# Two transformer blocks in float32 on one core: GpSimd sums the squares of tiles 0 to 13 for the four wide norms

## Chip, cores and metric

One Trainium2 chip, one core. The time is the device time of one launch in microseconds (us), measured from outside; a profiled execution also has a span, from its first to its last instruction. Lower is better.

## What is computed

A sequence of 256 tokens of width 2048 passes through two blocks, all in float32. The first has an RMS norm, an input projection, sparse attention beside a gated convolution, an output projection, a second RMS norm and a convolutional feed-forward part. The second has an RMS norm, latent and differential attention, gates, an output projection, an RMS norm and a gated feed-forward part. A last RMS norm closes the program. The part that matters here:

```
def rms_norm(x, g):
    xf = x.astype(jnp.float32)
    y = xf * lax.rsqrt(jnp.mean(xf * xf, axis=-1, keepdims=True) + NORM_EPS)
    return (y * g.astype(jnp.float32)).astype(x.dtype)

x = x + jnp.concatenate([attn, conv], axis=-1) @ w_out[l]
h = rms_norm(x, ffn_norm_g[l])
x = x + conv_glu_ffn(h, w_up[l], ffn_conv_w[l], ffn_conv_b[l], w_down[l])
...
return rms_norm(x, final_norm_g)
```

For each token the squares of 2048 values are added up. There are four such sums after large products: k = 1 (after `w_out`), k = 3 (after the first block's last down projection; two sums here, since the first block's final norm and the second block's first norm follow each other and are evaluated together), k = 4 (after `w_out_2`) and k = 5 (the last norm, after the second down projection).

## The kernel before

**Layout.** Activations stand transposed: channels on the 128 partitions, tokens along the free dimension. `x` is 16 tiles of 128 channels by 256 tokens. A matrix product is kept exact by splitting: each weight is `w_hi` + `w_lo` and each activation is a pair of halves side by side (`hp` or `yp`, 512 columns). One step of a product, called a pair below, is a 512-column product with `w_hi` (L1585) and a 256-column product with `w_lo` (L1586).

**The stream of weights.** Weights come in units of 128 x 1024 or 128 x 768 values. SyncE's queue loads a unit into one of four `w_raw` buffers, ScalarE copies it to `w_hi` (L540), VectorE (in the first phases GpSimd, L860) subtracts to get `w_lo` (L875), TensorE multiplies. Semaphores hand the four buffers round. TensorE's order is written out by phase (`gemm`, L1596): a step has two groups of output chunks, each group walks `nu` units, and `between` or `hooks` names work put ahead of unit `u` of group `g`.

**The wide norms.** The gains are applied before the sum is known, and the reciprocal root is multiplied in later, so that the next product need not wait. In the closing phase before each norm (`w_out`, `down1_2`, `w_out_2`, `down2_2`), VectorE adds each finished pair of chunks to `x` (L1241, L1242), ScalarE squares the pair of tiles into `sq` (L599; for k = 3 also `sq_g`, L602) and scales them for the next product (L604), VectorE forms the low half (L927, not for k = 5). All engines follow their own program order.

**The sum of squares** is TensorE's. A product with a 128 x 128 block of squares as the stationary operand and one column of ones gives 128 tokens' sums over 128 channels; it adds into columns of PSUM bank `STAT`. That is two products for each tile (`stats`, L1630; product at L1640), each issued as two instructions, after one 4-column product with zeros that starts the sum (L1633, also two instructions). Tiles 0 to 11 are read in `early` (L1616), hooked ahead of group 1, unit 0 of the last step of the closing phase; tiles 12 to 15 in `opening` (L1652), ahead of unit 1 of the next phase. For k = 5 `early` also transposes three pieces of the output (`out_turn`, L1623, transposes at L1561), and tiles 12 to 15 follow the last product. From the sum VectorE and ScalarE make the reciprocal root (`inverse_root`, L962, L593), and TensorE spreads it over the partitions (`spread`, L1645, L1650).

## Time and profile before

| | us |
|---|---|
| median of 3 runs (2957.24 to 2966.63) | 2958.05 |
| profiled execution, its own time | 2957.51 |
| its span | 2955.7 |
| TensorE busy in the span | 2898.1 (98%) |
| VectorE, ScalarE, GpSimd busy | 2092.1, 1375.9, 174.1 |

The span is 1.8 us shorter than the time of the same execution. TensorE is busy nearly throughout, so the question at each place is what it is busy with, and what it would wait for if that work went away. GpSimd works only in the first tenth of the span. A mean clock of 0.985 of full speed was granted to TensorE.

### The profile page before, as it was taken

What the parts mean: (1) busy time and instruction counts of PE and PEld (TensorE: products, weight loads), DVE (VectorE), ACT (ScalarE), POOL (GpSimd) and SP (SyncE); (2) the same over time, 40 slices, a digit from 0 to 9 for tenths busy, and PEclk for the clock granted to TensorE, in tenths of its full rate; (3) what the DMA queues carried; (4) which work ended last, traced back from release to release, by engine and by line L of the source; (5) the groups of instructions that cost most, each with busy time, mean ns of one, the idle gap of its engine ahead of it and who ended that gap; (6) DMA issues with size and microseconds to landing.
All of it is one profiled execution on the core that took longest, in us unless ns stands there. A gap on an engine that the chain in (4) does not pass through costs nothing.

```text
span 2955.7 us, 50070 instructions
## 1 busy us (share of the span) xinstructions
PE 2898.1 (98%) x17096; PEld 2528.0 (86%) x17096; DVE 2092.1 (71%) x3291; ACT 1375.9 (47%) x1798; POOL 174.1 (6%) x81
## 2 busy tenths in 40 slices
PE   6998999999999999999999999999999999999998
PEld 5877888888888888888888888888888888888887
DVE  4986767876886786577776777777657766775674
ACT  3334746644554455445443454544445533343344
POOL 3865000000000000000000000000000000000000
PEclk9999999999999999899999999999999999999998
DMA  9655355665655555444556555555555566565553
GB/s 227 176 145 133 91 136 175 187 192 187 187 189 191 186 185 180 131 135 145 150 167 185 166 173 166 173 167 183 188 162 187 183 196 189 181 197 190 180 183 120
DMA packets 596731, 507.37 MB, mean 172 GB/s; under 512 B 90123, under 2 KB 594715, under 8 KB 596251
## 3 DMA queue, kind: packets, MB, share of 16 engines
q1 hardware_dynamic: 595040, 503.61, 56.6%
q0 software_dynamic: 560, 2.12, 0.2%
q8 instruction: 55, 0.90, 0.1%
q10 hardware_dynamic: 1035, 0.40, 0.1%
q14 instruction: 41, 0.34, 0.0%
HBM read 503.88 MB, written 2.12 MB: 171 GB/s over the span
## 4 chain that ended last, share of the span: by engine, by line
PE 92%; DVE 4%; ACT 2%; issue 1%; ACTq 0%; DMA 0%; DVEq 0%
PE banks L1585 57%; PE banks L1586 28%; PE banks L1640 2%; PE banks L1561 1%; DVE banks L1069 1%; ACT hp_f L660 1%; DVE arena L891 1%; PE banks L1903 0%; PE banks L1659 0%; PE banks L1956 0%; ACTq L520 0%; DVE hp_f L1160 0%; DVE arena L1187 0%; PE banks L1763 0%; PE banks L1906 0%
## 5 line engine op out<-in xcount | busy, mean ns | idle before, releaser
L1585 PE MATMUL banks<-hp,w_hi 128*128 128x512 f32 x4416 | 1567.2, 400 | 13.0 <-issue 10.0
L540 ACT ACTIVATE w_hi<-w_raw 128x1024 fp32r<-128x1024 f32 (+2 forms) x960 | 996.5, 1044 | 1193.4 <-PE banks L1586 1176.5
L875 DVE TENSOR_TENSOR w_lo<-w_raw,w_hi 128x1024 fp32r<-128x1024 f32 (+2 forms) x889 | 1061.3, 1206 | 567.6 <-ACT w_hi L540 550.0
L1586 PE MATMUL banks<-hp,w_lo 128*128 128x256 f32 x4416 | 1236.8, 280 | 0.0
L1585 PEld LDWEIGHTS banks<-hp,w_hi 128*128 128x128 f32 x4416 | 833.3, 189 | 211.5 <-issue 12.3
L1585 PE MATMUL banks<-yp,w_hi 128*128 128x512 f32 x2752 | 965.2, 397 | 4.1 <-DVE yp L1296 2.8
L1586 PEld LDWEIGHTS banks<-hp,w_lo 128*128 128x128 f32 x4416 | 836.8, 189 | 2.6 <-issue 1.9
L1586 PE MATMUL banks<-yp,w_lo 128*128 128x256 f32 x2752 | 767.2, 279 | 0.0
L1585 PEld LDWEIGHTS banks<-yp,w_hi 128*128 128x128 f32 x2752 | 518.3, 188 | 128.0 <-DVE yp L1296 3.8
L1586 PEld LDWEIGHTS banks<-yp,w_lo 128*128 128x128 f32 x2752 | 519.5, 189 | 0.1
L891 DVE TENSOR_REDUCE arena<-banks 128x256 f32<-128x512 f32 (+1 forms) x392 | 251.5, 684 | 86.0 <-PE banks L1586 84.7
L860 POOL TENSOR_TENSOR w_lo<-w_raw,w_hi 128x1024 fp32r<-128x1024 f32 x71 | 171.8, 2423 | 80.5 <-ACT w_hi L540 80.5
L1069 DVE SCALAR_TENSOR_TENSOR banks<-arena,vec,banks 128x256 f32<-128x256 f32 x232 | 102.0, 485 | 3.7
L1585 PE MATMUL banks<-arena_r,w_hi 128*128 128x512 f32 x272 | 101.0, 410 | 1.8 <-DVE arena L891 1.5
L992 DVE TENSOR_TENSOR arena<-arena,cst 128x512 f32<-128x512 f32 x128 | 88.5, 691 | 4.2
L1268 DVE SCALAR_TENSOR_TENSOR arena<-arena,vec 128x256 f32<-128x256 f32 x176 | 77.5, 482 | 17.2 <-ACT arena L722 11.3
L1586 PE MATMUL banks<-arena_r,w_lo 128*128 128x256 f32 x272 | 77.4, 285 | 0.0
L722 ACT ACTIVATE arena<-arena,vec 128x256 f32<-128x256 f32 x88 | 48.2, 595 | 52.7 <-DVE arena L992 52.7
L1241 DVE TENSOR_TENSOR x<-banks,x 128x256 f32<-128x256 f32 (+1 forms) x128 | 53.2, 416 | 23.5 <-PE banks L1586 23.5
L1585 PEld LDWEIGHTS banks<-arena_r,w_hi 128*128 128x128 f32 x272 | 52.3, 192 | 15.8 <-DVE arena L891 4.3
L712 ACT ACTIVATE arena<-arena 128x512 f32<-128x512 f32 x44 | 27.9, 633 | 80.6 <-DVE arena L992 61.4
L787 ACT ACTIVATE arena<-arena,small 128x128 f32<-128x128 f32 x64 | 31.5, 493 | 60.1 <-DVE small L1426 46.2
(255 smaller groups left out, 1565.5 us busy)
## 6 DMA issues: line engine op xcount, KB each, us to landing
w_raw<-in_w_in SPq DMA_DIRECT2D x480, 256.0 KB, 3.0
w_raw<-in_w_up SPq DMA_DIRECT2D x352, 256.0 KB, 2.9
w_raw<-in_w_ffn_up SPq DMA_DIRECT2D x176, 256.0 KB, 3.6
w_raw<-in_w_ffn_gate SPq DMA_DIRECT2D x176, 256.0 KB, 3.0
w_raw<-in_w_down SPq DMA_DIRECT2D x160, 256.0 KB, 3.0
w_raw<-in_w_ffn_down SPq DMA_DIRECT2D x160, 256.0 KB, 3.0
w_raw<-in_w_out SPq DMA_DIRECT2D x128, 256.0 KB, 3.1
w_raw<-in_w_mla_proj SPq DMA_DIRECT2D x64, 256.0 KB, 3.0
```

The costliest lines, as they stand in the source:

```text
L540: nc.scalar.activation(w_hi[:, s, 0:n], w_raw[:, s, 0:n], ACT.Copy).then_inc(hi_ready, 1)
L722: ins = nc.scalar.activation(dst[:, c, :], buf[:, c, FTAPS - 1:], ACT.Identity, scale=vdyn("ffn_conv_w", ch + (FTAPS - 1) * 2 * FT), bias= ...
L860: nc.gpsimd.tensor_tensor(w_lo[:, s, 0:n], w_raw[:, s, 0:n], w_hi[:, s, 0:n].bitcast(f32), ALU.subtract)\
L875: v.tensor_tensor(w_lo[:, s, 0:n], w_raw[:, s, 0:n], w_hi[:, s, 0:n].bitcast(f32), ALU.subtract)\
L891: v.tensor_reduce(dst, pair(b)[0:rows], X, ALU.add).then_inc(chunk_out, 1)
L992: return v.tensor_tensor(dst, dst, bcast(r_row, 2), ALU.mult)
L1069: ins = v.scalar_tensor_tensor(conv_y[:, t, :] if k == TAPS - 1 else acc, src, w, acc, ALU.mult, ALU.add)
L1241: link(v.tensor_tensor(xt, banks[:, c, 0:T], xt, ALU.add))
L1268: ins = v.scalar_tensor_tensor(dst[:, c, :], buf[:, c, k:k + T], vdyn("ffn_conv_w", at_ch[c] + k * 2 * FT), dst[:, c, :], ALU.mult, ALU.add)
L1585: mm(banks[:, b, :], w_hi[:, s, at:at + P], rhs[:, kt, :], start=kt == kt_first, stop=False)
L1586: ins = mm(banks[:, b, 0:T], w_lo[:, s, at:at + P], rhs[:, kt, 0:T], start=False, stop=kt == kt_last)
L1640: ins = mm(banks[:, STAT, at + b:at + b + 1], src[:, t, b * P:(b + 1) * P], ones[:, 0:1], start=False, stop=t == KT - 1, skip_group_check= ...
```

## The change

GpSimd adds, for each of k = 1, 3, 4, 5, tiles 2 and 3, then 4 and 5, up to 12 and 13 into tiles 0 and 1 of `sq`, in place: six additions of 128 x 512, each after the squares of its pair. For k = 3 the same is done for `sq_g`, the two chains by turns, so 30 additions in all. TensorE then reads tiles 0, 1, 14 and 15 alone. For k = 1, 3 and 4 it reads all four in `opening`, after all six additions (semaphore `summed`); `early` has nothing left for them. For k = 5 `early` is moved to unit 3 of group 1, with the transposes first and tiles 0 and 1 behind them, and tiles 14 and 15 follow the last product.

```diff
@@ gpsimd
+            for k in (1, 3, 4, 5):
+                for p in range(1, KT // 2 - 1):
+                    for src, name, done, nth in ((sq, "squares", "summed", NTH[k]), (sq_g, "squares_g", "summed_g", 0))[:2 if k == 3 else 1]:
+                        pool.wait_ge(sem(name), KT // 2 * (nth + 1) + p + 1 if nth or name == "squares" else 2 * p + 2)
+                        if p > 1:
+                            pool.wait_ge(sem(done), (KT // 2 - 2) * nth + p - 1)
+                        nc.gpsimd.tensor_tensor(src[:, 0:2, :], src[:, 0:2, :], src[:, 2 * p:2 * p + 2, :], ALU.add).then_inc(sem(done), 1)
@@ tensor, gemm
-                    step(whole, {(1, 0): lambda: early(k)})
+                    step(whole, {(1, nu - 1): lambda: early(k)})
@@ early
-                stats(k, 0, KT - 4)
                 if k == 5:
                     pe.wait_ge(sem("gained"), KT * NTH[k] + 8)
                     for j in range(3):
                         out_turn(j)
+                    stats(k, (0, 1))
@@ stats
-            def stats(k, t0, t1):
-                if t0 == 0:
+            def stats(k, tiles):
+                if 0 in tiles:
                     mm(banks[:, STAT, 0:4], ident, zeros, start=True, stop=False, skip_group_check=True)
...
-                    for t in range(t0, t1):
-                        pe.wait_ge(sem(name), nth + (t // 2 + 1 if nth else t + 1))
+                    for t in tiles:
+                        if t == 0:
+                            pe.wait_ge(sem(done), (KT // 2 - 2) * (NTH[k] + 1 if at == 0 else 1))
+                        if t == KT - 2:
+                            pe.wait_ge(sem(name), KT // 2 * (NTH[k] + 2) if at == 0 else KT)
@@ opening
-                return {(0, 1): lambda: stats(k, KT - 4, KT), at: lambda: spread(k)}
+                return {(0, 1): lambda: stats(k, (0, 1, KT - 2, KT - 1)), at: lambda: spread(k)}
@@ end
-            stats(5, KT - 4, KT)
+            stats(5, (KT - 2, KT - 1))
```

The first place is the last step of `w_out` on TensorE (k = 1). Before, the products on squares stand between its two groups; `squares` is ScalarE's semaphore, `chunk_out` VectorE's.

```order
L1585 MATMUL banks<-yp,w_hi 128x512
L1586 MATMUL banks<-yp,w_lo 128x256
L1633 MATMUL banks<-small,cst 128x4 [waits chunk_out]
L1640 MATMUL banks<-cst,arena 128x1 [waits squares]
L1640 MATMUL banks<-cst,arena 128x1
L1640 MATMUL banks<-cst,arena 128x1 [waits squares]
```

Now the sum begins behind the first unit of the next phase (L1593 and L1594 are L1585 and L1586 of before, L1641 and L1651 are L1633 and L1640):

```order
L1594 MATMUL banks<-hp,w_lo 128x256
L1641 MATMUL banks<-small,cst 128x4
L1651 MATMUL banks<-cst,arena 128x1 [waits summed]
L1651 MATMUL banks<-cst,arena 128x1 x3
L1651 MATMUL banks<-cst,arena 128x1 [waits squares]
L1651 MATMUL banks<-cst,arena 128x1 x3
L1593 MATMUL banks<-hp,w_hi 128x512 [waits lo_ready3,gained_lo]
```

Twenty-four products went, eight stand there as before, and the start of the sum moved past two units of `w_out` and one of the next phase. The second place is the last step of `down2_2` on TensorE (k = 5), now:

```order
L1594 MATMUL banks<-hp,w_lo 128x256
L1569 MATMUL banks<-cst,arena 128x128 [waits gained]
L1569 MATMUL banks<-cst,arena 128x128 x11
L1641 MATMUL banks<-small,cst 128x4
L1651 MATMUL banks<-cst,arena 128x1 [waits summed]
L1651 MATMUL banks<-cst,arena 128x1 x3
L1593 MATMUL banks<-hp,w_hi 128x512 [waits lo_ready3,mid]
```

Before, the start of the sum, 24 products and the 12 transposes stood ahead of the group's first unit; now 12 transposes, the start and 4 products stand ahead of its last.

On GpSimd the additions follow the last subtraction for the weights; the first rows are k = 1 and the beginning of k = 3:

```order
L860 TENSOR_TENSOR w_lo<-w_raw,w_hi 128x1024 [waits hi_ready] x71
L869 TENSOR_TENSOR arena<-arena 128x512 [waits squares]
L869 TENSOR_TENSOR arena<-arena 128x512 [waits summed,squares] x5
L869 TENSOR_TENSOR arena<-arena 128x512 [waits squares]
L869 TENSOR_TENSOR arena<-arena 128x512 [waits squares_g]
```

Nothing stood behind the subtractions before.

## Rows read from the trace of the kernel before

**Rows 1.** The page: busy time by engine, and the chain that ended last by line.

```profile
PE 2898.1 (98%) x17096; PEld 2528.0 (86%) x17096; DVE 2092.1 (71%) x3291; ACT 1375.9 (47%) x1798; POOL 174.1 (6%) x81
PE banks L1585 57%; PE banks L1586 28%; PE banks L1640 2%; PE banks L1561 1%; DVE banks L1069 1%; ACT hp_f L660 1%; DVE arena L891 1%; PE banks L1903 0%; PE banks L1659 0%; PE banks L1956 0%; ACTq L520 0%; DVE hp_f L1160 0%; DVE arena L1187 0%; PE banks L1763 0%; PE banks L1906 0%
```

**Rows 2.** Timeline, TensorE, k = 1: start us, us, engine, line, operation, count.

```profile
430.01 0.28 PE L1633 MATMUL banks<-small,cst 128*128 128x4 f32 x2
430.15 7.94 PE L1640 MATMUL banks<-cst,arena 128*128 128x1 f32 x48
...
448.71 1.84 PE L1640 MATMUL banks<-cst,arena 128*128 128x1 f32 x16
450.42 0.48 PE L1585 MATMUL banks<-hp,w_hi 128*128 128x512 f32 x1
```

**Rows 3.** Timeline, TensorE, k = 3.

```profile
1176.65 0.28 PE L1633 MATMUL banks<-small,cst 128*128 128x4 f32 x2
1176.79 17.38 PE L1640 MATMUL banks<-cst,arena 128*128 128x1 f32 x96
...
1206.94 3.63 PE L1640 MATMUL banks<-cst,arena 128*128 128x1 f32 x32
1210.43 0.48 PE L1585 MATMUL banks<-hp,w_hi 128*128 128x512 f32 x1
```

**Rows 4.** Timeline, TensorE, k = 4.

```profile
2172.80 0.28 PE L1633 MATMUL banks<-small,cst 128*128 128x4 f32 x2
...
2197.35 0.48 PE L1585 MATMUL banks<-yp,w_hi 128*128 128x512 f32 x1
```

**Rows 5.** Timeline, TensorE, k = 5 and the end.

```profile
2921.29 0.28 PE L1633 MATMUL banks<-small,cst 128*128 128x4 f32 x2
...
2928.82 2.80 PE L1561 MATMUL banks<-cst,arena 128*128 128x128 f32 x12
2931.28 0.78 PE L1585 MATMUL banks<-hp,w_hi 128*128 128x512 f32 x1
...
2941.30 0.95 PE L1640 MATMUL banks<-cst,arena 128*128 128x1 f32 x8
2943.88 1.05 PE L1640 MATMUL banks<-cst,arena 128*128 128x1 f32 x8 [1.64 <-ACT arena L599]
```

**Rows 6.** Windows, TensorE: stretch, length, busy (count), granted clock, DMA share, GB/s.

```profile
430.00:438.00 8.00, 8.00 (x53) 0.68 0.46 141
438.00:443.00 5.00, 5.00 (x16) 0.50 0.12 37
...
448.00:451.00 3.00, 3.00 (x25) 1.00 0.39 117
...
1211.00:1216.00 5.00, 5.00 (x22) 0.66 0.03 10
```

**Rows 7.** Windows, L1585 alone: the count is of pairs; columns as in rows 6.

```profile
700.00:800.00 100.00, 100.00 (x290) 1.00 0.60 188
...
2050.00:2150.00 100.00, 100.00 (x284) 1.00 0.58 187
```

**Rows 8.** One line of GpSimd: count, then min/median/max ns.

```profile
L860 POOL TENSOR_TENSOR w_lo<-w_raw,w_hi x71: 2335/2404/3965, 29.6 to 271.9; 128x1024 fp32r<-128x1024 f32 x71
```

**Rows 9.** Timelines of GpSimd and VectorE, a subtraction beside a VectorE operation, and without.

```profile
262.76 2.39 POOL L860 TENSOR_TENSOR w_lo<-w_raw,w_hi 128x1024 fp32r<-128x1024 f32 x1 [3.66 <-ACT w_hi L540]
...
262.89 4.41 DVE L1185 TENSOR_TENSOR arena<-arena,yp_f 128x2048 f32<-128x2048 f32 x1
...
279.80 2.28 DVE L1192 TENSOR_TENSOR arena<-arena,yp_f 128x2048 f32<-128x2048 f32 x1
```

**Rows 10.** Windows, VectorE, in the closings of k = 1 and 3; columns as in rows 6.

```profile
401.00:423.60 22.60, 18.65 (x33) 1.00 0.85 188
1140.00:1174.00 34.00, 23.83 (x40) 1.00 0.57 179
```

**Rows 11.** Timeline, ScalarE: the squares of the last pair, k = 1.

```profile
448.14 0.63 ACT L599 ACTIVATE arena<-x 128x512 f32<-128x512 f32 x1 [0.88 <-DVE x L1242]
```

More of the change, by code:

```diff
@@ L1628, in out_turn @@
                 ins.then_inc(sem("out_turned"), 1)
-            def stats(k, t0, t1):
-                if t0 == 0:
+            def stats(k, tiles):
+                if 0 in tiles:
                     mm(banks[:, STAT, 0:4], ident, zeros, start=True, stop=False, skip_group_check=True)
-                for src, name, at, nth in ((sq, "squares", 0, KT // 2 * (NTH[k] + 1)), (sq_g, "squares_g", 2, 0)):
+                for src, done, name, at in ((sq, "summed", "squares", 0), (sq_g, "summed_g", "squares_g", 2)):
                     if name == "squares_g" and k != 3:
                         continue
-                    for t in range(t0, t1):
-                        pe.wait_ge(sem(name), nth + (t // 2 + 1 if nth else t + 1))
+                    for t in tiles:
[3 more added lines that the diff above has]
+                            pe.wait_ge(sem(name), KT // 2 * (NTH[k] + 2) if at == 0 else KT)
                         for b in range(QB):
@@ L1641, in stats @@
                                      start=False, stop=t == KT - 1, skip_group_check=True)
-                if t1 == KT:
+                if KT - 1 in tiles:
                     ins.then_inc(sem("sums"), 1)
```

## The prediction

> **What bounds the kernel now.** I read the page first. TensorE is busy 98% of the span, and in the chain that ended last nearly everything is its own: the pairs of L1585 and L1586 make 85%, the products on squares (L1640) 2% [rows 1]. A step that leaves TensorE is thus worth its full length there, if the engine finds its next operands ready. So I read TensorE's timeline at the four norms. At each, the pairs stop and a run of one-column products stands between two of them, with no idle time printed: 48 instructions for k = 1 [rows 2], 96 for k = 3 [rows 3]; k = 4 and 5 are built as k = 1 [rows 4, 5]. The one wait is at the very end, 1.64 us for ScalarE's squares [rows 5].
>
> The reader should see two prices in these rows. The first is the products' own. In the short run behind the next phase's first unit, 16 instructions take 450.42 - 448.71 = 1.71 us, 0.107 us each [rows 2]. In the long run of k = 3, 96 take 17.24 us, 0.180 each [rows 3]. The second price explains the difference: the windows show the granted clock at 0.68 of full speed over the long run of k = 1, and then 0.50, the lower level of 1.2 GHz, for the 5 us after it, though the pairs are back by then [rows 6]. Between 438 and 443 only 16 records of TensorE's products stand, 8 pairs in 5 us, where 14 would fit. Behind the short run the clock is 1.00 [rows 6]. So a long run of one-column products also slows the products of full width that follow.
>
> **What a pair costs.** L1585 stands 290 times in 100 us of a feed-forward phase and 284 times in 100 us late in the second block, both at full clock [rows 7]: 0.345 and 0.352 us for a pair. Where it reads 0.345 and where 0.352 I can't derive. The timeline has the slower pace in all closing steps before the runs, so I use 0.352 there.
>
> **k = 1.** Before, from the start of the sum to the first pair behind the short run: 450.42 - 430.01 = 20.41 us [rows 2]. In it lie three units of 8 pairs. After, the same place holds 24 pairs by 0.352 = 8.45, the 4-column start of the sum (0.14, from 430.01 to 430.15) and 16 instructions, 1.71: together 10.30. Gain 10.1 us.
>
> **k = 3.** Before, 1210.43 - 1176.65 = 33.78 us [rows 3]. In it: four units of 6 pairs and one of 8. After: 32 by 0.352 = 11.26, 0.14, and 32 instructions as they are now, 1210.43 - 1206.94 = 3.49: together 14.89. Gain 18.9 us. The clock falls after this run now (0.66 over 1211 to 1216 [rows 6]), and will still: nothing gained or lost.
>
> **k = 4.** Before, 2197.35 - 2172.80 = 24.55 us [rows 4], with 40 pairs in it. After: 14.08 + 0.14 + 1.71 = 15.93. Gain 8.6 us.
>
> **k = 5.** Before, from 2921.29 to the last pair's end at 2941.30 [rows 5], 20.01 us, with 24 pairs. After: 8.45 for the pairs; 12 transposes, which take 2931.28 - 2928.82 = 2.46 us at about half clock, so 1.23 at full; 0.14; 8 instructions, 0.86: together 10.68. Gain 9.3 us. The products of tiles 12 and 13 behind the last pair (0.95 us) go too, but they lie in the wait for the last squares, 1.64 us more [rows 5]: worth nothing, since that wait grows by as much. The rest of the tail stays.
>
> **What hides the additions.** GpSimd is idle after 272 us [rows 8]. 1024 columns of two inputs take it 2.40 us there [rows 8]; 512 I put at half, 1.2 us, an estimate from that row; the bounds are below 1.2 on the one side and on the other 3.96, the longest for 1024. A closing phase gives one pair of tiles for each group of TensorE: every 5.65 us (16 pairs) for k = 1, 8.4 for k = 3, 11.3 for k = 4. One addition, or two for k = 3, fit. The last addition starts behind the squares of tiles 12 and 13, which follow the end of group 0 by about 4 us, and TensorE asks for the sum one group and one unit later, 8.5 us after that end for k = 1: 3 us are over. What is late next is as before ScalarE's last squares: for k = 1 they run 448.14 to 448.77 [rows 11], and the product that needs them, the ninth instruction of the run, starts near 449.6. Now the start of the sum stands ahead as well, so 0.9 us are over. Behind TensorE's new waits stand only its own pairs, and two more units wait prepared in the buffers.
>
> **What the additions cost VectorE.** This is the one place where the trace speaks against the change. VectorE's L1185 took 4.41 us while GpSimd's subtraction ran from 262.76 to 265.15; the like operation L1192 took 2.28 us alone [rows 9]. 265.15 + 2.28 is 267.43, about where L1185 ended (267.30): it stood until GpSimd was done. Both read two inputs from SBUF. L875 and L927, which VectorE runs in the closings, do so too. An addition may therefore hold VectorE for 1.2 us. In the closing of k = 1 VectorE is busy 18.65 of 22.60 us, in that of k = 3 23.83 of 34.00 [rows 10]: idle 3.95 and 10.2 us, against additions of 4 x 1.2 = 4.8 and 8 x 1.2 = 9.6. Only for k = 1 can VectorE fall behind, by 0.85 in 22.6 us, some 1.3 us over the six additions, and two units stand ready before TensorE would see it. I take 1 us for all of it, between 0 and 36 (30 additions, each passed on in full). "SBUF — State Buffer" of the Trainium skill (Who interferes with whom) says that a VectorE instruction with two SBUF inputs and a GpSimd instruction that reads SBUF exclude each other, the first to start holding the ports for the whole instruction. By that rule, which rows 9 bear out for this pair of instructions, VectorE's blocked time is up to the additions' whole length; without it one would put the cost at zero and the gain 1 us higher.
>
> **Sum.** 10.1 + 18.9 + 8.6 + 9.3 - 1 = 45.9, say 46 us. The profiled execution took 2957.5 us (span 2955.7 and 1.8 around it), 0.5 below the median of the runs. 2957.5 - 46 = **2911.5 us**.
>
> **Rivals.**
>
> *Another pace of the pairs.* The closings run at 0.352 a pair and the feed-forward phases at 0.345 [rows 7]. For k = 1 the quick pace is there as soon as the clock comes back behind the long run; for k = 4 only behind the spread's product, two units after the short run. If the long run is what sets the quick pace for k = 1, taking it away leaves the slow one until the next pause, at worst over the whole first feed-forward part. It reaches from 450 [rows 2] to the start of `down1_2`, seven groups of 8.4 us before 1176.65 [rows 3], so to about 1118: 668 x (290/284 - 1) = 14 us given back, 2925.5 us. For: the switch stands there. Against: for k = 4 a short run and a spread do it as well, and these remain for k = 1. The same might go the other way behind k = 3, where the slow pace stays. 0.17 for the loss, 0.05 for a gain of like size (2898).
>
> *The clock falls at the short runs too.* They grow from 16 to 18 instructions, 1.7 to 1.85 us; the clock held after 1.7 and fell after 3.5 [rows 6]. A fall costs 8 pairs at 5 us in place of 2.8: 2.2 us each for k = 1 and 4, and up to 1.7 for k = 5, whose run is 2.2 us: 2917.6 us. This lies inside the forecast's own range.
>
> *VectorE is held in full.* All 30 additions pass their length on: 36 us given back in place of 1, 2946.5 us, still faster. It would take VectorE being the bound, which rows 10 show only for k = 1. 0.03.
>
> *The additions are slow, and TensorE waits for them: slower than before.* In place, one waits for the one before, so a norm's chain is 6 (12) additions long. From the squares of pair 1 to TensorE's question there are for k = 1 five groups and 4 us, 32 us; for k = 3 five groups and 7.5, 49.5; for k = 5 some 46; for k = 4 64. At d us for an addition TensorE waits 6d - 32 for k = 1 and 12d - 49.5 for k = 3. The waits eat the 46 us from d = 7.1 on: 10.6 + 35.7. At 8 us it would be 16 + 46.5 + 2 = 64.5 us of waiting, 2976 us. For: no addition of this form is in the trace, and VectorE can hold GpSimd as well. Against: twice the columns took 2.40 us, and the longest, held by VectorE, 3.96 [rows 8]. 0.03.
>
> *The time only moves.* The stream of weights might fall behind a TensorE that no longer pauses. Against: two and more steps of each closing run now without a pause and without a wait, at a DMA share of 0.85 and 0.57 [rows 10]. 0.02, near 2955.
>
> **How the numbers follow.** Forecast 0.70, with its own range of 2905 to 2918.5 (a fall of the clock at all short runs above; below, the faster pace in the closings, no hold of VectorE). The slower pace 0.17, a faster 0.05, VectorE in full 0.03, slow additions 0.03, moved time 0.02. The range takes in the first two: 2904 to 2928. About 0.3%, or 9 us, is what a measurement of this kernel can tell from no change; all but slow additions and moved time are beyond it. Faster 0.96, same 0.02, slower 0.02 (one of the three for slow additions falls short of the point).
>
> **What would show it.** Right: no L1640 in the last steps of `w_out`, `down1_2`, `w_out_2`; 18 instructions in a run for k = 1 and 4 with granted clock 1.00 behind them; 30 additions near 1.2 us on GpSimd; no idle time of TensorE ahead of the run; some of VectorE's L875 and L927 up to 1.2 us longer where they meet an addition. Wrong: idle time of TensorE released by GpSimd or by VectorE in the closings, a run that starts late, or a count of L1585 near 284 in 100 us where it is 290 now.

## The result

| | before | after |
|---|---|---|
| median of the runs beside each other | 2960.68 us (4 runs, 2957.24 to 2966.63) | 2924.01 us (4 runs, 2919.20 to 2925.79) |
| profiled execution, its own time | 2957.51 | 2925.79 |
| its span | 2955.7 | 2924.0 |
| mean granted clock | 0.985 | 0.991 |

The ratio is 0.9868, with a 95% interval of 0.9852 to 0.9885: 36.7 us faster. A second measurement, the kernels in turn over five rounds (label changed_5), gave 2923.94 against 2962.49 us, ratio 0.9876 [0.9854, 0.9897]: 38.5 us faster. Predicted were 46 us and 2911.5; the time lies inside the range of 2904 to 2928, but 5.5 us above the forecast's own range of 2905 to 2918.5. It is inside only because the range also took in the rival of a slower pace. The direction and the places came as argued; 7.5 to 9 us of the gain did not come.

The page of the changed kernel, its busy times, the chain that ended last by line, and the additions as a group. It answers to [rows 1]:

```profile
PE 2865.1 (98%) x16856; PEld 2496.0 (85%) x16856; DVE 2105.3 (72%) x3291; ACT 1376.4 (47%) x1798; POOL 218.8 (7%) x111
...
PE banks L1593 56%; PE banks L1594 29%; PE banks L1569 1%; DVE banks L1077 1%; ACT hp_f L660 1%; DVE w_lo L883 1%; DVE arena L899 1%; PE banks L1914 0%; PE banks L1670 0%; ACT w_hi L540 0%; DMA cst<-tables 0%; PE banks L1967 0%; DVE hp_f L1168 0%; DVE arena L1195 0%; PE banks L1651 0%
...
L869 POOL TENSOR_TENSOR arena<-arena 128x512 f32<-128x512 f32 x30 | 44.7, 1500 | 2582.9 <-ACT arena L599 2582.9
```

TensorE lost 240 instructions and 33 us of busy time; the products on squares (now L1651) fell from 2% of the chain to 0. VectorE has the same 3291 instructions and 13 us more in them; without the additions (no_adds, below) it is back at 2092.9, so they come with the additions. GpSimd's additions take 1.50 us on average; I had put 1.2.

TensorE's timeline at the four norms (start us, us, engine, line, shape, count, and in brackets the idle time before it and what ended it), to be laid beside [rows 2 to 5]. The breaks stand between k = 1, 3, 4 and 5:

```profile
442.43 0.28 PE L1641 MATMUL banks<-small,cst 128*128 128x4 f32 x2
442.57 1.03 PE L1651 MATMUL banks<-cst,arena 128*128 128x1 f32 x8
444.42 1.05 PE L1651 MATMUL banks<-cst,arena 128*128 128x1 f32 x8 [0.82 <-ACT arena L599]
445.33 0.77 PE L1593 MATMUL banks<-hp,w_hi 128*128 128x512 f32 x1
...
1192.46 1.03 PE L1651 MATMUL banks<-cst,arena 128*128 128x1 f32 x8
1194.56 3.74 PE L1651 MATMUL banks<-cst,arena 128*128 128x1 f32 x24 [1.07 <-ACT arena L599]
...
2173.03 1.93 PE L1651 MATMUL banks<-cst,arena 128*128 128x1 f32 x16
2174.81 0.48 PE L1593 MATMUL banks<-yp,w_hi 128*128 128x512 f32 x1
...
2905.12 1.47 PE L1569 MATMUL banks<-cst,arena 128*128 128x128 f32 x12
...
2906.57 1.03 PE L1651 MATMUL banks<-cst,arena 128*128 128x1 f32 x8
...
2912.26 1.05 PE L1651 MATMUL banks<-cst,arena 128*128 128x1 f32 x8 [2.43 <-ACT arena L599]
```

All long runs are gone, and the transposes of k = 5 run at full pace (1.47 us for 12, before 2.80). But for k = 1 and k = 3 the run is cut in two: TensorE stands 0.82 and 1.07 us for ScalarE's squares of the last pair. No such wait stood there before. The wait at the very end grew from 1.64 to 2.43 us, by 0.8 where the prediction had 0.95.

The windows over and behind the runs of k = 1, 3 and 4 (stretch, length, then busy us and count of TensorE, its weight loads, VectorE, ScalarE and GpSimd, then granted clock, DMA share, GB/s):

```profile
440.00:445.00 5.00, 4.18 (x30) 3.77 (x30) 4.93 (x9) 2.18 (x4) 0.24 (x1) 1.00 0.83 255
445.00:450.00 5.00, 5.00 (x23) 4.35 (x23) 3.02 (x10) 2.60 (x4) 0.00 (x0) 0.66 0.42 137
...
1198.00:1203.00 5.00, 5.00 (x17) 4.32 (x17) 3.75 (x18) 1.35 (x3) 0.00 (x0) 0.50 0.01 4
...
2175.00:2180.00 5.00, 5.00 (x29) 4.34 (x29) 3.48 (x9) 3.61 (x4) 0.00 (x0) 1.00 0.26 89
```

Behind k = 1 the clock falls to 0.66, though the run has the same 18 instructions as that of k = 4, behind which it stays at 1.00. The difference that the rows show between the two is the pause in the middle.

**Where the time went.** I cut both executions at the same places of TensorE's timeline: the first pair of `w_out` and of `down1_2`, the first product of each spread, two starts of steps in the second block, the first pair of `down2_2`, and the end. Differences, before less after:

| stretch | before | after | gained | predicted |
|---|---|---|---|---|
| start to first pair of `w_out` | 390.34 | 392.75 | -2.41 | 0 |
| to the spread of k = 1 | 65.72 | 59.79 | 5.93 | 10.1 |
| to the first pair of `down1_2` | 667.50 | 676.58 | -9.08 | 0 |
| to the spread of k = 3 | 96.95 | 79.82 | 17.13 | 18.9 |
| to a step in the second block | 299.88 | 297.41 | 2.47 | 0 |
| to its last step before `w_out_2` | 482.61 | 482.62 | -0.01 | 0 |
| to the spread of k = 4 | 200.08 | 191.58 | 8.50 | 8.6 |
| to the first pair of `down2_2` | 665.10 | 665.10 | 0.00 | 0 |
| to the end (k = 5) | 87.52 | 78.35 | 9.17 | 9.3 |

The sum is 31.70, the difference of the spans. The four norms gave 40.7 of the predicted 47, and the first feed-forward part ran 9.1 us slower with the same instructions; the start and the second block, -2.4 and 2.5, cancel. Two shortfalls are thus to be explained: the waits and the clock for k = 1 and 3, and those 9 us. These are differences of two single executions; how much of each row an execution can shift by itself is seen in the table of all twelve, below.

### The profile page after: what moved, and what is told of

Read it like the earlier page. It is cut to its first block, busy times and chain, and to the rows that moved or that the text cites. A ratio compares the mean times of both kernels' runs of the same rounds, so it can differ in the third digit from the quotient of the medians.

```text
span 2924.0 us, 49646 instructions
## 1 busy us (share of the span) xinstructions
PE 2865.1 (98%) x16856; PEld 2496.0 (85%) x16856; DVE 2105.3 (72%) x3291; ACT 1376.4 (47%) x1798; POOL 218.8 (7%) x111
## 3 DMA queue, kind: packets, MB, share of 16 engines
q0 software_dynamic: 560, 2.12, 0.2%
HBM read 503.88 MB, written 2.12 MB: 173 GB/s over the span
## 4 chain that ended last, share of the span: by engine, by line
PE 91%; DVE 5%; ACT 2%; issue 1%; DMA 1%; DVEq 0%; SPq 0%; ACTq 0%
PE banks L1593 56%; PE banks L1594 29%; PE banks L1569 1%; DVE banks L1077 1%; ACT hp_f L660 1%; DVE w_lo L883 1%; DVE arena L899 1%; PE banks L1914 0%; PE banks L1670 0%; ACT w_hi L540 0%; DMA cst<-tables 0%; PE banks L1967 0%; DVE hp_f L1168 0%; DVE arena L1195 0%; PE banks L1651 0%
## 5 line engine op out<-in xcount | busy, mean ns | idle before, releaser
L1593 PE MATMUL banks<-hp,w_hi 128*128 128x512 f32 x4416 | 1573.0, 400 | 13.0 <-issue 10.0
L883 DVE TENSOR_TENSOR w_lo<-w_raw,w_hi 128x1024 fp32r<-128x1024 f32 (+2 forms) x889 | 1071.6, 1217 | 531.9 <-ACT w_hi L540 513.9
L1594 PE MATMUL banks<-hp,w_lo 128*128 128x256 f32 x4416 | 1241.5, 281 | 0.0
L1593 PEld LDWEIGHTS banks<-hp,w_hi 128*128 128x128 f32 x4416 | 833.6, 189 | 213.2 <-issue 12.3
L1593 PE MATMUL banks<-yp,w_hi 128*128 128x512 f32 x2752 | 964.9, 395 | 3.8 <-DVE yp L1304 2.5
L1594 PEld LDWEIGHTS banks<-hp,w_lo 128*128 128x128 f32 x4416 | 838.7, 190 | 2.6 <-issue 1.9
L1594 PE MATMUL banks<-yp,w_lo 128*128 128x256 f32 x2752 | 771.8, 280 | 0.0
L1593 PEld LDWEIGHTS banks<-yp,w_hi 128*128 128x128 f32 x2752 | 516.6, 188 | 125.0 <-DVE yp L1304 3.5
L1594 PEld LDWEIGHTS banks<-yp,w_lo 128*128 128x128 f32 x2752 | 520.5, 189 | 0.1
L869 POOL TENSOR_TENSOR arena<-arena 128x512 f32<-128x512 f32 x30 | 44.7, 1500 | 2582.9 <-ACT arena L599 2582.9
L1593 PE MATMUL banks<-arena_r,w_hi 128*128 128x512 f32 x272 | 100.3, 408 | 1.8 <-DVE arena L899 1.5
L1276 DVE SCALAR_TENSOR_TENSOR arena<-arena,vec 128x256 f32<-128x256 f32 x176 | 77.6, 482 | 17.1 <-ACT arena L722 11.3
L1594 PE MATMUL banks<-arena_r,w_lo 128*128 128x256 f32 x272 | 77.1, 283 | 0.0
L1593 PEld LDWEIGHTS banks<-arena_r,w_hi 128*128 128x128 f32 x272 | 51.9, 191 | 15.7 <-DVE arena L899 4.4
```

The source lines that it names most:

```text
L869: nc.gpsimd.tensor_tensor(src[:, 0:2, :], src[:, 0:2, :], src[:, 2 * p:2 * p + 2, :], ALU.add).then_inc(sem(done), 1)
L883: v.tensor_tensor(w_lo[:, s, 0:n], w_raw[:, s, 0:n], w_hi[:, s, 0:n].bitcast(f32), ALU.subtract)\
L1276: ins = v.scalar_tensor_tensor(dst[:, c, :], buf[:, c, k:k + T], vdyn("ffn_conv_w", at_ch[c] + k * 2 * FT), dst[:, c, :], ALU.mult, ALU.add)
L1593: mm(banks[:, b, :], w_hi[:, s, at:at + P], rhs[:, kt, :], start=kt == kt_first, stop=False)
L1594: ins = mm(banks[:, b, 0:T], w_lo[:, s, at:at + P], rhs[:, kt, 0:T], start=False, stop=kt == kt_last)
```

## The experiments

Each kernel is compared with the kernel before, run beside it on the same chip. The chips differ between the experiments, so times of kernels that did not run side by side are compared by their distance to the kernel before. On the waits two theories stand against each other: **the hold**, by which the additions hold VectorE, so that its `x` and ScalarE's last squares come late; and **the lost pause**, by which TensorE no longer gives the others time ahead of the opening, whoever adds. On the slow feed-forward part: it is **the change's doing**, since the long run is gone (the prediction's rival), or **it is not**, and the pace varies by itself.

### The changed kernel again (again)

No edit.

> The changed kernel, executed again. Theory 1 (the pace of the pairs, 0.347 or 0.353 us, is set by chance at each pause): another profile shows the two paces over other stretches; the stretch from the first spread product to the last pair of the second up/down pair, 0.353 from 630 on in the first profile, may read 0.347 all through; time 2914 to 2928. Theory 2 (the change itself leads to the slow pace there): the same pattern again, 0.353 from 630 to 1128, time within 1 us of 2925.8. Both: the stretch between the spread of k = 4 and the first pair of down2_2 is 665.1 us.

Measured: 2924.57 us, ratio 0.988 [0.9864, 0.9897]. Both waits are there (0.79 and 1.06), and the slow feed-forward part too: 676.56 us. The stretch of k = 1 was 58.23 in place of 59.79; the first profile has 1.5 us of low clock just behind the start of `w_out` (five pairs at 0.64 us from 394.3 on), which the repetition has not. So the k = 1 stretch gained 7.5 here and 5.9 there, the 1.5 us being an accident of the clock ahead of the place in question. It is not the change's: the second execution of the kernel before has it too, at 394.0, and so have changed_5 and double_adds.

On the feed-forward part this run spoke for the change's doing: the slow stretch came again in the same place.

### Without the additions (no_adds)

```diff
-            for k in (1, 3, 4, 5):
-                ...
-                        nc.gpsimd.tensor_tensor(src[:, 0:2, :], src[:, 0:2, :], src[:, 2 * p:2 * p + 2, :], ALU.add).then_inc(sem(done), 1)
@@ stats
-                            pe.wait_ge(sem(done), (KT // 2 - 2) * (NTH[k] + 1 if at == 0 else 1))
+                            pe.wait_ge(sem(name), (KT // 2 * (NTH[k] + 2) - 1) if at == 0 else KT - 2)
```

> The changed kernel without GpSimd's 30 additions; TensorE reads tiles 0, 1, 14 and 15 alone, so tiles 2 to 13 are left out of the sums. Theory 1: VectorE is no longer held in the closings, the waits for ScalarE's squares ahead of the ninth instruction at the openings of k = 1 (0.82 us) and k = 3 (1.07 us) shrink to at most 0.3 us, and with them goes the fall of the clock behind k = 1 (2.2 us): 3 to 5 us less from the pairs of w_out to the spread of k = 1, 4 to 6 us in all, beside the chance of the pace. Theory 2 (the additions held VectorE so far that TensorE lost the 15 us that the prediction misses): 12 to 15 us less, and shorter closings. Theory 3 (the waits come from the missing pause alone, since ScalarE and VectorE used it to catch up): the waits stay.

Measured: 2921.22 us, ratio 0.9859 [0.9842, 0.9877]. Its TensorE for k = 1 (here L1635 is the start of the sum, L1645 the product) and the window behind it:

```profile
441.25 0.28 PE L1635 MATMUL banks<-small,cst 128*128 128x4 f32 x2
441.39 1.93 PE L1645 MATMUL banks<-cst,arena 128*128 128x1 f32 x16
443.17 0.48 PE L1587 MATMUL banks<-hp,w_hi 128*128 128x512 f32 x1
```

```profile
443.00:448.00 5.00, 5.00 (x30) 4.40 (x31) 2.98 (x9) 2.53 (x4) 0.00 (x0) 1.00 0.42 120
```

The wait is gone, and with it the fall of the clock. The stretch is 55.81 us, a gain of 9.9 over the first profile of before, against the 10.1 predicted. (Over k3_only, where k = 1 is untouched and the stretch is 64.17, it is 8.4.) VectorE's timelines say why. With the additions (changed kernel, first profile):

```profile
433.39 1.85 DVE L935 SCALAR_TENSOR_TENSOR hp<-x,vec,hp 128x256 fp32r<-128x256 f32 x2
...
436.74 4.59 DVE L883 TENSOR_TENSOR w_lo<-w_raw,w_hi 128x1024 fp32r<-128x1024 f32 x3
...
442.04 0.41 DVE L1249 TENSOR_TENSOR x<-banks,x 128x256 f32<-128x256 f32 x1
```

with these two additions beside them on GpSimd:

```profile
433.03 1.53 POOL L869 TENSOR_TENSOR arena<-arena 128x512 f32<-128x512 f32 x1 [4.21 <-ACT arena L599]
438.70 1.55 POOL L869 TENSOR_TENSOR arena<-arena 128x512 f32<-128x512 f32 x1 [4.13 <-ACT arena L599]
```

and without additions (L929 and L877 are L935 and L883):

```profile
432.22 0.88 DVE L929 SCALAR_TENSOR_TENSOR hp<-x,vec,hp 128x256 fp32r<-128x256 f32 x2 [1.85 <-ACT hp L604]
...
434.61 3.57 DVE L877 TENSOR_TENSOR w_lo<-w_raw,w_hi 128x1024 fp32r<-128x1024 f32 x3
...
438.89 0.41 DVE L1243 TENSOR_TENSOR x<-banks,x 128x256 f32<-128x256 f32 x1
```

The two L935 take 0.97 us longer and the three L883 1.02: two additions passed on 2.0 us. TensorE's last group of `w_out` ended near 439.6 with the additions and 438.4 without (start of the sum less one unit of 8 x 0.353). VectorE took up that group's result 2.4 us after its end in the first case, 0.5 us in the second: the same 2 us. The last squares ended at 441.22 without additions, 1.0 us before the ninth instruction of the run would ask for them (441.39 + 8 x 0.107), and at 444.37 with them, 0.9 us after it did (442.57 + 8 x 0.107). For k = 1 the hold thus explains the wait, once the long run no longer covers it, and the rule quoted from the Trainium skill in the prediction ("SBUF — State Buffer", Who interferes with whom) agrees with these rows.

For k = 3 it does not. Without the additions TensorE still waits 0.69 us:

```profile
1186.48 1.03 PE L1645 MATMUL banks<-cst,arena 128*128 128x1 f32 x8
1188.21 5.00 PE L1645 MATMUL banks<-cst,arena 128*128 128x1 f32 x24 [0.69 <-ACT arena L599]
```

ScalarE and VectorE ahead of it (same kernel):

```profile
1181.68 3.16 ACT L540 ACTIVATE w_hi<-w_raw 128x1024 fp32r<-128x1024 f32 x3
1187.52 0.63 ACT L599 ACTIVATE arena<-x 128x512 f32<-128x512 f32 x1 [2.69 <-DVE x L1244]
```

```profile
1182.76 2.36 DVE L877 TENSOR_TENSOR w_lo<-w_raw,w_hi 128x1024 fp32r<-128x1024 f32 x2 [2.12 <-ACT w_hi L540]
1185.03 0.87 DVE L929 SCALAR_TENSOR_TENSOR hp<-x,vec,hp 128x256 fp32r<-128x256 f32 x2
1185.83 0.42 DVE L1243 TENSOR_TENSOR x<-banks,x 128x256 f32<-128x256 f32 x1
```

ScalarE has two sorts of squares to make for each pair of tiles here and does its copies for the weights behind them; VectorE waits 2.12 us for those copies, and comes to the last group's result 2.3 us after its end (near 1183.5). In the kernel before, ScalarE stood idle for 20.3 us while the long run went on, and everything was in time. That is the lost pause. It is read from these rows; no run gave the pause back without the products. Shown is that most of the wait stays without the additions. The whole run then took longer than in the changed kernel (5.00 us for 24 instructions, not 3.74), since the clock fell within it: the mean over 1186 to 1193 is 0.68. So this kernel loses 4.0 us for k = 3 (1.5 of them by pairs at 0.64 us from 1121 on, just behind the first pair of `down1_2`, where the repetition has none) and wins 2.4 for k = 1 and 5.0 in the feed-forward part (671.60 us) over the repetition; its total says little of what the additions cost, its k = 1 says it plainly.

### The sum begun in two halves (split_opening)

```diff
-                return {(0, 1): lambda: stats(k, (0, 1, KT - 2, KT - 1)), at: lambda: spread(k)}
+                return {(0, 1): lambda: stats(k, (0, 1)), (0, 2): lambda: stats(k, (KT - 2, KT - 1)), at: lambda: spread(k)}
```

> The changed kernel with the opening in two: the start and tiles 0 and 1 ahead of unit 1 of the next phase, tiles 14 and 15 ahead of unit 2. Theory 1: no wait for the squares, and no run is longer than 1.9 us, so the clock stays at 1.00 behind k = 1 and behind k = 3: 0.8 + 2.2 us less for k = 1, 1.1 + 2.2 us for k = 3, about 6 us in all beside the chance of the pace. Rival (the clock falls by the sum of both runs, or the reciprocal root comes late to the spread): the fall stays behind k = 3, or TensorE waits up to 3 us at the spread of k = 1, and the time is that of the changed kernel.

Measured: 2914.21 us, ratio 0.9841 [0.9819, 0.9863]; again in five rounds, below. TensorE for k = 1 and k = 3:

```profile
440.19 1.03 PE L1651 MATMUL banks<-cst,arena 128*128 128x1 f32 x8
...
444.00 0.95 PE L1651 MATMUL banks<-cst,arena 128*128 128x1 f32 x8
...
1187.62 1.93 PE L1651 MATMUL banks<-cst,arena 128*128 128x1 f32 x16
...
1192.31 1.84 PE L1651 MATMUL banks<-cst,arena 128*128 128x1 f32 x16
```

and the windows behind each:

```profile
445.00:450.00 5.00, 5.00 (x29) 4.37 (x29) 4.49 (x13) 4.12 (x5) 0.00 (x0) 1.00 0.28 90
...
1194.00:1199.00 5.00, 5.00 (x30) 4.34 (x30) 3.89 (x18) 3.20 (x5) 0.00 (x0) 1.00 0.00 0
```

With all 30 additions in place there is no wait at either norm, the clock stays at 1.00, and the stretches are 55.81 and 75.48 us: 2.4 and 4.2 less than in the repetition. The additions hold VectorE as before (their median is 1.46 us), but now it has a unit more of time. So the price of the additions is the wait and the fall of the clock behind it, not VectorE's time as such. The rivals of the expectation did not come: the clock stays up behind k = 3 too, and TensorE does not wait at the spread. The feed-forward part was slow here as well (676.57), so the gain is not from there. Between medians it is 10.4 us over the repetition, of which the two stretches hold 6.6.

### Only k = 3, and only k = 1, changed (k3_only, k1_only)

Both are the kernel before, with the additions, the shorter sum and the opening of one norm:

```diff
-                stats(k, 0, KT - 4)
+                if k != 3:
+                    stats(k, 0, KT - 4)
...
-                return {(0, 1): lambda: stats(k, KT - 4, KT), at: lambda: spread(k)}
+                return {(0, 1): lambda: stats3() if k == 3 else stats(k, KT - 4, KT), at: lambda: spread(k)}
```

(`stats3` is the changed kernel's `stats` for this norm; k1_only is the same with 1 for 3.)

> The kernel before with the change for k = 3 alone. The sum of the prediction gives k = 3 18.9 us; the first profile of the change shows 17.1 between the first pair of down1_2 and the spread of k = 3. Theory 1: that stretch is 79 to 82 us (97.4 before), k = 1, 4 and 5 as before, and the time is 2940 to 2946, with a part of up to 10 us to either side from the pace. Rival (the places depend on each other, a pause removed at one is made good at the next): less than 14 us in the stretch.

> The kernel before with the change for k = 1 alone. If what is done for k = 1 brings the slow pace of 632 to 1129, this kernel shows it (676.6 us from the spread of k = 1 to the first pair of down1_2), and about 7 us of gain at k = 1 less 9 us, so 2958 to 2964, no better than before. If the pace is chance: 667.5 in some executions, time 2949 to 2956. Either way the wait for the squares at the opening, 0.8 us, and the clock's fall behind it, as in the changed kernel.

Measured: k3_only 2946.52 us, ratio 0.9954 [0.9937, 0.997], just above the expected 2946, its k = 3 stretch 80.73 and its wait 0.84. In medians it gained 15.3 us of the 18.9 predicted. k1_only 2957.50 us, ratio 0.9978 [0.9965, 0.9991], over ten runs: 6.4 us. That falls between its two expectations. Its stretch is 58.08 (7.6 gained), its wait 1.49 us where 0.8 was expected, and the clock behind it 0.66:

```profile
439.01 1.03 PE L1663 MATMUL banks<-cst,arena 128*128 128x1 f32 x8
441.54 1.05 PE L1663 MATMUL banks<-cst,arena 128*128 128x1 f32 x8 [1.49 <-ACT arena L599]
```

The longer wait goes with a quicker closing: here the pairs of `w_out` started 0.347 us apart, in every other execution 0.353, and VectorE took up the last group's result 3.1 us after its end in place of 2.4. Both norms thus show their shortfall alone, without the other.

On the feed-forward part k3_only, which keeps the long run of k = 1, was quick (667.51). k1_only, which lacks that run, was slow from 627 to 900 us and quick from there (672.47); no_adds, which lacks it too, was quick until 893 and slow from there (671.60). The slow pace is thus not tied to one place, but so far every kernel without the long run had some of it.

### The kernel before once more (before_again), and extra products (nudges)

> The kernel before, profiled once more. Open is whether the pace of the pairs is drawn anew at each pause in each execution, or belongs to the program. By chance: the pace between 456 and 1123 (0.347 all through in the first profile, 667.5 us from the spread to the first pair of down1_2) and the time to the first pair of w_out (390.3) differ by 2 us or more. By program: 667.5 and 390.3 within 0.5 us.

Measured: 2971.02 us in one run (the highest of the 13 runs beside k1_only is 2967.47), span 2969.2. This execution of the unchanged kernel, long run and all, has the slow feed-forward part: 676.57 us, and 101.45 for the stretch of k = 3. The start took 392.80 us, not 390.34. Both differences are the ones expected if the pace is chance. Pairs alone in the same 100 us, in this execution (L1585), then in the changed kernel (L1593); the count behind the busy time is that of pairs, the next two numbers are their weight loads:

```profile
700.00:800.00 100.00, 100.00 (x284) 53.18 (x283) 1.00 0.60 185
```

```profile
700.00:800.00 100.00, 100.00 (x284) 53.18 (x283) 1.00 0.59 184
```

The first profile of before has 290 there [rows 7]. So the change is not needed for the slow pace, and the count varies in one and the same kernel. The pace changes at a pause. After one in the first feed-forward part, before `yp` of L1296 (L1304), the first profile of before went on quickly and the changed kernel slowly, with the same pause of 0.26 us:

```profile
634.40 0.50 PE L1585 MATMUL banks<-yp,w_hi 128*128 128x512 f32 x1 [0.26 <-DVE yp L1296]
634.86 0.40 PE L1585 MATMUL banks<-yp,w_hi 128*128 128x512 f32 x1
635.21 0.39 PE L1585 MATMUL banks<-yp,w_hi 128*128 128x512 f32 x1
```

```profile
630.90 0.50 PE L1593 MATMUL banks<-yp,w_hi 128*128 128x512 f32 x1 [0.26 <-DVE yp L1304]
631.35 0.40 PE L1593 MATMUL banks<-yp,w_hi 128*128 128x512 f32 x1
631.70 0.40 PE L1593 MATMUL banks<-yp,w_hi 128*128 128x512 f32 x1
```

Behind its first pair the one starts its pairs 0.35 us apart and the other too: the two paces, 0.347 and 0.353, differ by less than such a row can show. The counts over 100 us show it, and it stays so for hundreds of us.

nudges is split_opening with a 4-column product ahead of seven units of the first step of the first block's second up projection, to break the stream there:

```diff
+            def nudge():
+                mm(banks[:, STAT, 8:12], ident, zeros, start=True, stop=True, skip_group_check=True)
...
-                    gemm(f"up{blk}_{p}", h, KT, normed(k), opening(k, (0, 3)) if p == 0 else {})
+                    gemm(f"up{blk}_{p}", h, KT, normed(k), opening(k, (0, 3)) if p == 0 else {(g, u): nudge for g in range(2) for u in range(4) if g or u} if p == 1 and blk == 1 else {})
```

> The kernel with the opening in two, and seven extra 4-column products (0.14 us each) in the first step of up1_1, one ahead of every unit but the first, where the slow pace (0.353) stood from the pause at 626 on in its first profile. If any small break of the row of pairs can reset the pace, it turns to 0.347 behind one of the seven and, if every break draws anew, may turn back behind another; with 0.347 from there to 1124 the stretch to down1_2 is 668 to 670 us in place of 676.6. If only a pause resets it, the slow pace holds through all seven and the stretch is 677.6.

Measured: 2917.51 us in one run. The pace was slow from 630 us through six of the seven extra products and turned quick at the seventh, at 730. Pairs in 80 us before and after them:

```profile
640.00:720.00 80.00, 79.72 (x226) 42.29 (x225) 1.00 0.59 186
740.00:820.00 80.00, 80.00 (x232) 43.23 (x232) 1.00 0.60 186
```

By 900 it was slow again, and the stretch as a whole came to 675.05, 1.5 us better than in split_opening. A break in the stream can change the pace but does not choose it. What does choose it stays open.

### The additions done twice (double_adds)

```diff
                         nc.gpsimd.tensor_tensor(src[:, 0:2, :], src[:, 0:2, :], src[:, 2 * p:2 * p + 2, :], ALU.add).then_inc(sem(done), 1)
+                        nc.gpsimd.tensor_tensor(src[:, 0:2, :], src[:, 0:2, :], src[:, 2 * p:2 * p + 2, :], ALU.add).then_inc(sem(done + "_a"), 1)
+                        pool.wait_ge(sem(done + "_a"), (KT // 2 - 2) * nth + p)
```

> The changed kernel with every addition of GpSimd done twice (so tiles 2 to 13 enter the sums twice). If an addition holds VectorE for its length, VectorE falls behind by 1.3 to 1.5 us more for each: the wait for the squares at the opening of k = 1 grows from 0.8 to 2 to 5 us, idle time of TensorE released by VectorE may appear in the closing of w_out, and the stretch from the pairs of w_out to the spread of k = 1 grows from 58.2-59.8 to 61 to 65 us; k = 4 and 5 stay. If additions only delay themselves: the stretch stays within 1 us.

Measured: 2943.76 us, ratio 0.9934 [0.9917, 0.9951], 20.1 us faster than the kernel before, where the changed kernel is 38.5 faster: 18.4 us lost. The waits of TensorE from 300 us on (us in total, times, longest), of this kernel and of the changed one:

```profile
PE banks L1653 <- ACT arena L599: 11.2, 3, 5.7
PE banks L1595 <- DVE w_lo L885: 6.9, 7, 1.8
```

```profile
PE banks L1651 <- ACT arena L599: 4.3, 3, 2.4
```

The waits for the squares are 3.07 us for k = 1 (2 to 5 expected) and 5.74 for k = 3. The stretches of k = 1 and k = 3 grew to 66.77 (65 at most expected) and 94.95; those of k = 4 (191.58) and k = 5 (78.31) did not move. Where the closing is long (k = 4) or nothing is halved for a next product (k = 5), doubled additions hide completely; for k = 1 and k = 3 the room is used up, and the second half of the doubled work costs 8.5 us (against the repetition) and 15.3. In each of these 1.5 us are the accident of the clock just behind a first pair, which the repetition has in neither place, so 7.0 and 13.8. VectorE's busy time shows the dose: 2092.9 us without additions, 2103.2 with them (repetition), 2129.4 with twice as many. The cost is steep once VectorE's idle time is gone.

This execution also speaks on the feed-forward part. It lacks the long run of k = 1, and was quick all through, 667.52 us:

```profile
700.00:800.00 100.00, 100.00 (x290) 54.14 (x289) 1.00 0.61 189
```

So the long run is not needed for the quick pace, as the change is not needed for the slow one. The three executions with the long run were quick, quick and slow; of the nine without it one was quick throughout, four slow in one of two parts, one slow but for the stretch behind the seventh extra product, three slow from 630 on. That the change shifts the odds is not excluded.

### Five rounds of the two best (changed_5, split_5)

> The changed kernel in more rounds, beside the next kernel on the same chip. If the pace of the pairs is drawn in each execution, runs spread over some 10 us around 2924, and the distance to the kernel before is 37 to 41 us between medians.

> The kernel with the opening in two, in more rounds. From its profile: 2.4 to 4.0 us less than the changed kernel at k = 1 and 4.2 us less at k = 3, so 6.5 to 8 us less between medians, 2915 to 2918 us. If the first four runs were favoured by the pace, the distance to the changed kernel is under 4 us.

Measured side by side: 2923.94 (2923.34 to 2927.66), ratio 0.9876 [0.9854, 0.9897], and 2914.17 (2912.94 to 2915.59), ratio 0.9838 [0.9817, 0.9859]. The runs of the two do not overlap: beginning the sum in two halves is worth about 10 us more, and beats both kernels. 6.5 to 8 were expected. In these two profiles the stretches of k = 1 and k = 3 hold 5.2 us of it (59.80 to 55.80, 78.25 to 77.02); where the rest comes from is not shown.

All twelve executions side by side, us; an asterisk marks a norm that is as in the kernel before:

| execution | k = 1 | first feed-forward | k = 3 | k = 4 | k = 5 |
|---|---|---|---|---|---|
| before | 65.72* | 667.50 | 96.95* | 200.08* | 87.52* |
| before_again | 65.62* | 676.57 | 101.45* | 201.67* | 85.95* |
| k3_only | 64.17* | 667.51 | 80.73 | 199.76* | 84.88* |
| k1_only | 58.08 | 672.47 | 98.31* | 200.07* | 84.84* |
| after | 59.79 | 676.58 | 79.82 | 191.58 | 78.35 |
| again | 58.23 | 676.56 | 79.69 | 191.48 | 77.22 |
| changed_5 | 59.80 | 672.47 | 78.25 | 191.48 | 78.27 |
| no_adds | 55.81 | 671.60 | 83.68 | 191.58 | 78.29 |
| split_opening | 55.81 | 676.57 | 75.48 | 191.58 | 78.30 |
| split_5 | 55.80 | 672.47 | 77.02 | 191.58 | 78.27 |
| nudges | 55.81 | 675.05 | 75.42 | 191.58 | 77.23 |
| double_adds | 66.77 | 667.52 | 94.95 | 191.58 | 78.31 |

Only k = 4 hardly depends on the execution once it is changed. The 1.5 us of low clock behind a first pair are in k = 1 of after, before_again, changed_5 and double_adds, and in k = 3 of before_again, k1_only, no_adds, double_adds and split_5. For k = 5 the pairs of `down2_2` ran at 0.347 in place of 0.353 in again, k3_only, k1_only and nudges, which is worth 1.1 us.

## Why the prediction was right, and what it mis-sized

**The two prices of a long run: right in kind.** The sum charged the one-column products for their own time and for the clock behind them. For k = 4 it met the trace in size too: 8.50 for 8.6, and 8.2 to 10.2 over all pairs of executions. For k = 5 (9.17 for 9.3) and for k = 1 without additions (9.9 for 10.1) the close match is partly luck. Both sums were taken from an execution in which these two places cost about 1.5 us more than in the others: k = 1 took 65.72 us there, against 64.17 in k3_only and 65.62 with 1.5 of accident in before_again; k = 5 took 87.52, against 85.95 in before_again, whose closing has the same pace. Against those the gains are 8.4 and 7.6 us. The prediction read one execution and gave the clock no spread.

**Inside the range, by the wrong rival.** The forecast's own range ended at 2918.5. What held the measured 2924 was the rival of the slower pace at 2925.5, and the cause that it gave did not hold (below). Between the two profiled executions 14.3 of the 46 us are missing: 9.1 by the slow pace, 4.2 at k = 1 (1.5 of accident, 2.4 by the additions), 1.8 at k = 3, 0.2 at k = 4 and 5, less the 1 us that was charged for the additions.

**The term of 1 us for all that the additions cost: mis-sized.** They cost 2.4 us at k = 1 alone. The mechanism was named, and the estimate of VectorE being 1.3 us behind was near (2.0 for the last two additions). The step that failed is "two units stand ready before TensorE would see it". That counted the weights alone. What TensorE saw first was not `w_lo` but the squares of the last pair, for which the prediction's own margin was 0.9 us (1.0 in no_adds). 2.0 us of hold against it leave about 1, and the wait printed is 0.8 us. Second, the wait was priced nowhere with its consequence: a run cut by a pause was followed by a clock of 0.66, 1.5 us more in the pairs behind it. Together 2.4 us for k = 1 (58.23 to 55.81), shown by no_adds and split_opening.

**k = 3: a check left out.** The prediction worked out the margin of the last squares for k = 1 alone. For k = 3 it was negative, mostly without the additions' help: 0.69 us of wait without them, 1.07 with. The forecast of 18.9 less the wait is 17.8, measured 17.1; as the stretch of before came out at 96.95 to 101.45, that closeness says little. It also called the fall of the clock behind the 34 instructions unavoidable; with the run in halves it does not fall, and split_opening passes the forecast there (21.5 us).

**Size of an addition: off, without effect.** Half of 2.40 gave 1.2; the shortest was 1.28, the mean 1.50. The last addition for k = 1 ended at 440.25, 2.3 us before TensorE asked (3 predicted). The rival of slow additions needed 7.1 us; double_adds, at 3.3 us for the two together (1.631 and 1.626), shows that long before that point VectorE is what suffers, which that rival had left out.

**The rival of another pace: seen, and not for the reason given.** The slow pace did stand in the first feed-forward part, from 631 to 1129 us, and took 9.1 us, where the rival had 14 for the whole part. The reason given, that the long run sets the quick pace, fell: the kernel behind the removed run started quickly and changed at a pause at 631, an execution of the kernel before did the same, and double_adds, without the run, stayed quick. What chooses the pace stays open. The base was low in turn: the profiled 2957.5 us was a quick execution, the medians of before being 2960.7 in the first comparison and 2961.9 to 2963.9 in the later ones. That is 3 us and more of the 12.5 by which the time was missed. Measured from the medians the gain is 38.5 us (36.7 the first time), and split_5, with neither wait nor fall of the clock, reaches 48.3.

**The rival of the clock falling at short runs** had 2.2 us for each fall where 1.5 were measured, and it came for k = 1, with the pause, and not for k = 4. **Moved time** did not come: in the trace of after TensorE waits for no weights from 300 us on.

## What to carry over

Work that leaves the bounding engine for an idle one is paid at full length only if every hand-over behind it keeps its margin, so work out that margin at each site, including what the removed pause had been giving the other engines. An idle engine whose instructions lengthen those of a nearly full one is not free: count its time against that one's idle time in each stage. A profile of one execution carries accidents of clock and pace of some us; profile the base twice before adding up gains of that size. Where a short wait stands in a chain of small products, move only those that need the late operand one step on; here that was worth 10 us between medians.

## What the runs showed of the hardware

**A pause in a short run goes with a lower clock behind it.** Sixteen one-column instructions in one piece left it at 1.00 in all nine cases (k = 4 in the eight kernels that change it; k = 1 without additions). The same number cut by a wait of 0.8 to 3.1 us had a fall within it or right behind it in all five (k = 1 in after, again, changed_5, k1_only, double_adds), to 0.66 over 5 us in the first. In halves with pairs between them (split_opening, split_5, nudges) they left it at 1.00. I had expected only length to matter.

**Identical pairs have two paces at full clock.** 0.347 and 0.353 us, 290 and 284 in 100 us, with the granted clock at 1.00 and no wait in either. The pace holds for hundreds of us and changes at breaks in the stream; the same place of the same kernel showed both. Up to 9 us of the first feed-forward part hang on it; what sets it stays open.

**GpSimd and VectorE lengthen each other.** Additions of one form took 1.28 to 2.03 us, and 2.35 at most when doubled. VectorE's two-input operations beside them took up to 1.1 us more than alone (2.32 for 1.22 us of 128x1024), and half of them nothing more: 30 additions, 44.7 us in all, lengthened VectorE's work by 10 to 12 us.
